# Gate tiles loaded in quarters, and ScalarE's queue loading the second product's first operands

## What is computed

```
def peer_ffn(h, w_q, subkeys, u, v):          # in chunks of tokens ht
    q = (ht @ w_q).reshape(PEER_CHUNK, PEER_HEADS, 2, PEER_HALF)
    s = jnp.einsum('thpc,hpnc->thpn', q, subkeys)
    sv, si = lax.top_k(s, PEER_TOPK)
    ...
    expert = jnp.take_along_axis(cand_i, top_pos, axis=-1)
    gate = jax.nn.softmax(top_s, axis=-1)
    act = jax.nn.gelu(jnp.einsum('thkd,td->thk', u[expert], ht), approximate=False)
    return jnp.einsum('thk,thkd->td', (gate * act), v[expert])
```

## Time and profile before

| | |
|---|---|
| time, median of 3 runs | 2747.01 us (2740.32 to 2752.84) |
| the profiled execution | 2750.26 us, its span 2748.1 us |
| TensorE busy | 2616.9 us, 95% |
| VectorE busy | 2140.3 us, 78% |
| ScalarE busy | 882.0 us, 32% |
| GpSimd busy | 1497.1 us, 54% |
| DMA | 763.30 MB, mean 278 GB/s |

### The profile page before, as it was taken

How to read it: one execution, slowest core, us unless ns; L and a number is a source line. 1 busy time by engine, 2 the same in 40 slices (tenths; PEclk the granted TensorE clock), 3 DMA queues, 4 the chain that set the end, 5 groups by cost and what they waited for, 6 DMA issues and landing times.

```text
span 2748.1 us, 41486 instructions
## 1 busy us (share of the span) xinstructions
PE 2616.9 (95%) x15177; PEld 2345.7 (85%) x15177; DVE 2140.3 (78%) x4568; ACT 882.0 (32%) x1654; POOL 1497.1 (54%) x960
## 2 busy tenths in 40 slices
PE   7999989999999999999999999988999989999988
PEld 6777758999999999989999999966877877878777
DVE  6022273599888999989999994278998988989987
ACT  4223242222122122246666662232222222222222
POOL 1111020346666677776555556546766766867762
PEclk9999999999999999999999999999999999999999
DMA  4110022335777788889999999999999999999995
GB/s 145 46 31 26 21 76 102 114 110 170 271 259 271 270 273 294 288 274 384 375 369 383 381 381 329 329 339 382 386 387 384 391 373 385 390 372 389 382 378 198
DMA packets 294988, 763.30 MB, mean 278 GB/s; under 512 B 24272, under 2 KB 114768, under 8 KB 292048
## 3 DMA queue, kind: packets, MB, share of 16 engines
q0 software_dynamic: 110592, 402.70, 39.2%
q1 hardware_dynamic: 166992, 296.21, 31.7%
q10 hardware_dynamic: 17280, 62.92, 5.9%
HBM read 669.47 MB, written 92.27 MB: 277 GB/s over the span
## 4 chain that ended last, share of the span: by engine, by line
PE 52%; DVE 16%; DMA 12%; issue 5%; POOL 2%; ACT 1%; another core or an unknown queue 0%; DVEq 0%; SPq 0%; ACTq 0%
PE bank L1553 23%; DMA a_raw<-act_d 11%; PE bank L1920 9%; PE wide L1920 8%; PE bank L1891 5%; DVE u_row L1358 4%; PE bank L1819 3%; PE bank L1802 2%; POOL w_lo L653 1%; DVE rest_k L1285 1%; DVE ix L1288 1%; DVE eq L1345 1%; DVE v_lo L1502 1%; DVE ix L1291 1%; DVE top L1286 1%
## 5 line engine op out<-in xcount | busy, mean ns | idle before, releaser
L704 POOL DMA_INDIRECT d_row<-in_v,ids x384 | 632.0, 1646 | 295.6 <-DVE yg L1495 207.6
L1553 PE MATMUL bank<-h_hi,w_hi 128*128 128x320 f32 (+1 forms) x2368 | 563.6, 319 | 14.0 <-POOL w_lo L653 11.9
L653 POOL TENSOR_TENSOR w_lo<-w_raw,w_hi 128x1024 fp32r<-128x1024 f32 x144 | 365.2, 2537 | 336.6 <-ACT w_hi L923 276.4
L1553 PE MATMUL bank<-h_hi,w_lo 128*128 128x320 f32 (+1 forms) x2368 | 547.2, 312 | 0.0
L1553 PE MATMUL bank<-h_lo,w_hi 128*128 128x320 f32 (+1 forms) x2368 | 546.8, 312 | 0.0
L1358 DVE CUSTOM_DVE_ANT_0 u_row<-wide,u_row 128x1024 f32<-128x1024 f32 x384 | 450.3, 1221 | 78.2 <-DMA u_row<-in_u_rows,ids 75.9
L1495 DVE SCALAR_TENSOR_TENSOR yg<-d_row,uh,yg 128x1024 f32<-128x1024 f32 x384 | 474.2, 1280 | 0.0
L662 POOL DMA_INDIRECT u_row<-in_u_rows,ids x384 | 392.9, 1023 | 111.8 <-issue 77.0
L1553 PEld LDWEIGHTS bank<-h_hi,w_hi 128*128 128x128 f32 x2368 | 394.2, 190 | 18.8 <-POOL w_lo L653 13.5
L1553 PEld LDWEIGHTS bank<-h_lo,w_hi 128*128 128x128 f32 x2368 | 400.4, 189 | 2.5
L1553 PEld LDWEIGHTS bank<-h_hi,w_lo 128*128 128x128 f32 x2368 | 399.1, 189 | 2.5
(11 more groups left out here) (227 smaller groups left out, 4267.0 us busy)
## 6 DMA issues: line engine op xcount, KB each, us to landing
w_raw<-in_u SPq DMA_DIRECT2D x128, 512.0 KB
v_raw<-in_v ACTq DMA_DIRECT2D x120, 512.0 KB
act_d<-act_st SPq DMA_DIRECT2D x128, 320.0 KB
g_d<-g_st SPq DMA_DIRECT2D x20, 2048.0 KB
a_raw<-act_d SPq DMA_DIRECT2D x160, 256.0 KB
g_raw<-g_d SPq DMA_DIRECT2D x32, 1024.0 KB
w_raw<-in_w_q SPq DMA_DIRECT2D x32, 512.0 KB
w_raw<-in_w_in SPq DMA_DIRECT2D x20, 512.0 KB
```

Source lines behind the costliest of these rows:

```text
L653: nc.gpsimd.tensor_tensor(w_lo[:, s % 2, :], w_raw[:, s % 2, :], w_hi[:, s % 2, :], ALU.subtract).then_inc(lo_done, 1)
L704: nc.gpsimd.indirect_dma_start(d_row[k % DR][:, :], None, v_rows, bass.IndirectOffsetOnAxis(ids[:, c:c + 1], 0)).then_inc(d_in[k % DR], 16)
L1553: ins = pe.matmul(banks[h][:, 0:n], lhs[:, part], rhs[:, k, h * n:(h + 1) * n], start=(k == 0 and lhs is lhs_hi and rhs is h_hi), stop=(k ...
```

## The change

Gates of tokens 0 to 511 are loaded in four transfers of 256 KB a half, four strips each, where one transfer of 1 MB was (`G_PART` is 4 strips, `G_PARTS` is 4). VectorE waits for all four of a half. In SyncE's loop the quarters of the next group's first half are asked for in steps 4 to 7, those of the second half in steps 8 and 9 and in steps 0 and 1 of the group that uses them; `g_first` in step 3 instead of 2. SyncE no longer loads ahead in the last six bodies of the first product. ScalarE's queue does: its 20 last items are unrolled, and behind each of items 128 to 142, after Gelu and `w_hi`, it issues one step of `fetch`: six units, four quarters, `g_first`, four quarters, one a step, with a `v_raw` ahead of it in steps 0, 1, 5, 6, 10 and 11. The first step waits for the stores of the gates and of the first chunks of `act_d`. The loading functions now take the queue as an argument.

```diff
+        def load_g(queue, g, s, q):
+            j, b = GT * g + VJ * s, G_PART * q
+            if g:
+                queue.wait_ge(pd_done, unit_of(g - 1, VJ * s + VJ - 1) + 1)
+            queue.dma_start(g_raw[s][:, b:b + G_PART, :], g_d[b:b + G_PART, :, j:j + VJ, :]
+                            .rearrange("b p j t -> p b (j t)")).then_inc(g_in[s], 16)
...
                     if n + AR + 1 < N_UNITS:
-                        load_a(n + AR + 1)
-                    if g + 1 < NG:
-                        if u == 2:
-                            load_first(g + 1)
-                        elif u == 4:
-                            load_g(g + 1, 0)
-                        elif u == 8:
-                            load_g(g + 1, 1)
+                        load_a(sp, n + AR + 1)
+                    if g and u < 2:
+                        load_g(sp, g, 1, u + 2)
+                    elif g + 1 < NG and u == 3:
+                        load_first(sp, g + 1)
+                    elif g + 1 < NG and 4 <= u < 8:
+                        load_g(sp, g + 1, 0, u - 4)
+                    elif g + 1 < NG and u >= 8:
+                        load_g(sp, g + 1, 1, u - 8)
...
-            with act.Fori(C0, ITEM_BODIES - 1) as it:
-                for s in range(2):
-                    chunk(it, s)
-            for s in range(2):
-                chunk(ITEM_BODIES - 1, s, ahead=False)
+            def fetch(n):
+                if n == 0:
+                    for k in range(2):
+                        act.wait_ge(g_out[k], 16 * PAIRS)
+                    for k in range(2):
+                        act.wait_ge(act_out[k], 16 * GT // 2)
+                if n % 5 < 2:
+                    act.dma_start(v_raw[:, 2 * (n // 5) + n % 5, :], v[2 * (n // 5) + n % 5, :, :]
+                                  ).then_inc(v_in[2 * (n // 5) + n % 5], 16)
+                if n < AR:
+                    load_a(act, n)
+                elif n < AR + G_PARTS:
+                    load_g(act, 0, 0, n - AR)
+                elif n == AR + G_PARTS:
+                    load_first(act, 0)
+                else:
+                    load_g(act, 0, 1, n - AR - G_PARTS - 1)
+
+            fetches = AR + 2 * G_PARTS + 1
+            chunks = 2 * (ITEM_BODIES - C0)
+            for n in range(chunks):
+                chunk(C0 + n // 2, n % 2, ahead=n + 2 < chunks)
+                if 0 <= n - (chunks - 1 - fetches) < fetches:
+                    fetch(n - (chunks - 1 - fetches))
...
-                        dve.wait_ge(g_in[j // VJ], 16 * (g + 1))
+                        dve.wait_ge(g_in[j // VJ], 16 * G_PARTS * (g + 1))
```

More of the change, by code:

```diff
@@ L67 @@
 RA = 5
+G_PART = 4
+G_PARTS = 4
 UNIT = 512
@@ L450, in build, with load_a, load_first @@
         LO_BANKS = 2 * NT
+        def load_a(queue, n):
+            g, j, f = unit(n)
+            if n >= AR:
+                queue.wait_ge(pd_done, n - AR + 1)
+            if f is None:
+                queue.dma_start(a_raw[:, n % AR, :], act_d[GT * g + j, :, 0:UNIT]).then_inc(a_in[n % AR], 16)
+            else:
+                j0 = GT * g + VJ * f
+                queue.dma_start(a_raw[:, n % AR, :].rearrange("p (j t) -> p j t", j=VJ),
+                                act_d[j0:j0 + VJ, :, FIRST * P:DS].rearrange("j p t -> p j t")
+                                ).then_inc(a_in[n % AR], 16)
+        def load_g(queue, g, s, q):
[4 more added lines that the diff above has]
+                            .rearrange("b p j t -> p b (j t)")).then_inc(g_in[s], 16)
+        def load_first(queue, g):
+            if g:
+                queue.wait_ge(pd_done, first_of(g - 1, 1) + 1)
+            queue.dma_start(g_first[:, :, :], g_d[UNIT // TW:STRIPS, :, GT * g:GT * g + GT, :]
+                            .rearrange("b p j t -> p b (j t)")).then_inc(gf_in, 16)
         @block.sync
@@ L544, in load_v @@
                 sp.dma_start(v_raw[:, j % VR, :], v[j, :, :]).then_inc(v_in[j % VR], 16)
[L546 to L572, removed]
             for it in range(C0, ITEM_BODIES):
@@ L581, in _ @@
                         store_strip(STRIPS - 1)
[L582 to L598, removed]
             store_item(ITEMS - 1)
@@ L611, in _ @@
                 sp.dma_start(y[i][:, :], x1_d[i]).then_inc(y_in, 16)
-            load_a(AR)
+            load_a(sp, AR)
             for g in range(NG):
```

## The result

The changed kernel took 2757.15 us (median of 20 runs, 2748.77 to 2765.48), the kernel before 2743.56 us beside it (20 runs, 2739.53 to 2752.84): a ratio of 1.0046 with a 95% interval of 1.0036 to 1.0056, some 13 us. The forecast was 9 us less. The profiled execution took 2760.79 us, and its span is 10.6 us longer than that of before; the profiled executions lie 6.7 us (before) and 3.6 us (changed) over their medians, so the difference between them is a little small. TensorE is busy as long as it was in the earlier trace rows.

What follows compares the result with a forecast made beforehand. Full DMA engines were taken to bound the second product's groups. Spreading -8.5 us and the items -0.5 us gave -9 us: from a median of 2747.0 to 2738 us, range 2722 to 2760 us.

Steps and rivals of the forecast that it cites:

- the term of -8.5 us for spreading: Groups of the second product: quarters spread over steps save 8.5 us, two thirds of the 12.5 us allowed at most.
- the best pair of neighbours: Group stretches 1953.2 to 2068.1 us: 389.3 GB/s against a mean of 383; at that rate the groups take 805.5 us.
- Nothing moves: Rival, groups of the second product: the rate sets the pauses, quarters only redistribute them, 0 to -2 us, 2746 us; chance 0.12.
- The rival of late quarters: Third and seventh unit of each group: the last quarter comes too late, +25 us, 2772 us; chance 0.11.
- Its threshold: Late quarters decide once the last lands more than 2.4 us after VectorE asks, over 24 us after its issue.
- a queue with less in it: SyncE's queue in the groups: argument against late quarters, beside a byte-set rate and longer pauses giving that queue the engines.
- Its price: Late quarters make each group take 60.2 us, 14 groups 843 us, +25 us.
- The 0.5 us of the items: Last 19 items of the first product: 134.71 us against 133.8; moving first loads off SyncE's queue gains 0.5 us.
- Issue times: Sign of being right: SyncE's units issue in under 5 us, ScalarE's issues take under 0.6 us.
- Some 2.4 us of a VectorE wait are absorbed: Stretch 2007.6 to 2068.1: TensorE misses 3.1 us for VectorE's 5.5, so only a longer wait pauses it.
- Bytes and packets stay: Loop over groups: quarters keep bytes and 512-byte packets, adding only 6 issues, 2.6 us a group, on SyncE.
- The fit of 2.0 us + bytes / 436 GB/s: Skill page's transfer cost: four quarters 10.4 us against 4.4 a half, some 190 us over 32 halves; the trace disagrees.

Runs made afterwards that it cites:

- 7 steps: Changed kernel with all four quarters of a half asked for back to back in steps 4 and 8, g_first in 2: 2743.18 us, 0.9993 of the kernel before.
- 6 steps: Changed kernel with two quarters in each of steps 4, 5, 8 and 9, g_first in 2: 2743.61 us, 0.9995 of the kernel before.
- 5 steps: Changed kernel with only the last quarter of each half one step earlier (steps 6 and 0): 2750.9 us, 1.0021 of the kernel before.
- 3 steps: Changed kernel with every quarter and g_first in the loop one step later: 2769.2 us, 1.0095 of the kernel before.
- half rows: Gathered rows cut to 2 KB in both kernels, VectorE adding that half twice: 2688.88 us in the order before, 2687.97 us in the changed one.

## Why the prediction held in some steps and failed in others

By notice, the ratios line up: 7 steps 0.9993, 6 steps 0.9995, 5 steps 1.0021, 4 steps 1.0046 (1.0035 without ScalarE's part), 3 steps 1.0095. Six and seven are alike; below that a step costs 0.25% at first and 0.5% at the end. **The cause is shown:** the last quarter of each half is asked for in step 7 or in step 1, and SyncE's queue, behind full engines, needs longer than the four steps that are left. The run at notice 5 moves that quarter alone and takes back half of the loss; how the other half divides between the notice and the step of `g_first` is open.

Point by point:

- *Right:* the engines are full (with half rows both orders take 54.4 us a group); ScalarE's issues are hidden (at most 0.67 us, a little over the 0.6 given as a sign, in an item's idle 5.33); the second product starts when it did; small transfers have no cost of their own here. The time, 2757 us, lies inside the range given, near its upper end, but on the other side of the kernel before than was forecast: 9 us less were forecast and 13 more measured. The 0.5% named as what a measurement can tell was too coarse: 0.46% is clear of an interval of 0.1% to either side.
- *The step that failed is the term of -8.5 us for spreading, wrong in sign and in kind.* The quarters in the loop alone cost 0.35% (some 9 us) where they were to bring 8.5. The term took the best pair of neighbours as a rate that a smoother order could hold. Quarters at once and pairs, which differ in the spread and by one step of notice, both stay within 0.1% of the kernel before and still wait 61 and 68 us. The low slices behind the pauses were read as bytes that a smoother order would bring back; no order brought the pauses down. What order can do is lower the rate: 378 GB/s instead of 383. "Nothing moves", at 0.12, is the rival that best describes spreading with a notice of six or seven steps.
- *The rival of late quarters, at 0.11, was the one that came true.* Its place (third and seventh unit) holds, though the waits of before stood there too: the prediction puts both of its two at the third unit, but the one ahead of 2112.47 is at the seventh. Its threshold, a landing over 24 us after the issue, was passed (27.49, 28.88) but was set too high: it took 22 us for four steps, and in group 1 VectorE was ready after 17.8; the chain also runs over a landing of 21.44 us. What failed is the conclusion from "a queue with less in it". The queue did take its transfers more readily; the issues of units in these stretches (min, median and max in ns, with their first and last start) before and now:

```profile
L552 SPq DMA_DIRECT2D a_raw<-act_d x112: 327/673/23377, 1837.9 to 2651.1; - x112
L461 SPq DMA_DIRECT2D a_raw<-act_d x112: 340/571/10419, 1837.7 to 2662.6; - x112
```

But it moves as many bytes a group as before, and in group 1 the quarter still came 9.78 us late: a unit issued 1.84 us behind it took 9.59 us to issue. So a long pause that "gives SyncE's queue the engines alone" didn't save it either.

- *Its price was too high:* +25 us from every group pausing as 2007.6 to 2128.0 did; measured +11.7. Seven of the 14 stretches take 59.8 us or more, but the other seven take 55.3 to 57.9. A long pause is often followed by a short group (61.0, then 55.3; together 116.3, and 116.0 before), which I read as the queues catching up in the pause; that is not shown. One step of notice more or less would have changed the price by half or doubled it (the runs with 5 and 3).
- *The 0.5 us of the items:* measured 134.50 against 134.71 us, too small to tell.
- *Issue times:* SyncE's units were to stay under 5 us; they reach 10.4 us. The waits were to stay under 4 us each; they average 80.0 / 13 = 6.2 us. Groups 2 to 14 were to take 55 to 59.5 us, and six take more; the rate was to be 386 to 390 GB/s, and no slice under 340, where the lowest shown here has 276.
- *"Some 2.4 us of a VectorE wait are absorbed" was misread.* It compares idle time alone. In 2007.6 to 2068.1 TensorE's 241 matmuls took 57.42 us at a granted clock of 0.94, and 54.40 us at 1.00 in 1953.2 to 2007.6; the stretch is 6.1 us longer than the full one, for a VectorE wait of 5.5. So a pause of TensorE brings slower matmuls behind it too: in 1885 to 1890 (below) the granted clock is 0.50, the lower of its two levels, after a slice in which TensorE was busy for 1.52 of 5 us.
- *"Bytes and packets stay":* the bytes do; the packets of the 14 stretches are 163380 instead of 161967, nearly all of the new ones under 512 bytes. Quarters at once have them too and cost nothing.
- *The fit of 2.0 us + bytes / 436 GB/s:* the Trainium skill, "DMA: Bandwidth & Descriptors", gives it in the section "Anatomy of one DMA — SWDGE (gpsimd) path", not in "Bandwidth", and for transfers on GpSimd's path. The quarters go by SyncE's and ScalarE's queues.

How a shorter notice lowers the rate of a stage that moves the same bytes is argued, not shown: during a VectorE wait for gates, no row is added, so no buffer for a row or a `v` comes free, so the engines run out of requests. The slices of the changed kernel that follow such waits agree in part: the rate is low in all three, from 395 GB/s at a share of 1.05 in 1875 to 1880, but the share has fallen only in the second and third (5 us each, columns as above):

```profile
1880.00:1885.00 5.00, 1.52 (x7) 0.94 (x5) 2.54 (x4) 0.63 (x1) 0.00 (x0) 0.92 1.04 320
1885.00:1890.00 5.00, 0.22 (x1) 0.22 (x2) 5.00 (x6) 0.00 (x0) 3.87 (x4) 0.50 0.98 323
...
2395.00:2400.00 5.00, 1.26 (x6) 0.72 (x4) 4.79 (x6) 1.58 (x2) 0.90 (x1) 0.96 0.88 276
```

GpSimd, which asks for the rows, does nothing from 1880 to 1885, TensorE almost nothing from 1885 to 1890. What would have shown it is a version with more buffers for rows at the same notice, which was not run.

## What to carry to other kernels

In a stage that fills the DMA engines, the deadline of an operand is that of its last byte: measure how long the queue takes from issue to landing under load (here 16.5 us in the median and up to 29), and ask for the last part at least that long ahead. Cutting a transfer into parts is safe where the last part is asked for no later than the whole was, and a loss where spreading pushes it back. If no order gives less time, look at the bytes: here a cut in them (which leaves out part of the result) gave 53 us, while none of the nine orders run, the changed kernel's among them, gave any.

## What was not expected of the hardware

- A quarter of 256 KB takes 16.5 us from issue to landing (median, quarters at once) with the engines full, and 5.4 us at a share of about 0.9 beside gathered rows of half the length. The share is an eighth lower and the bytes of the 14 stretches 29% fewer (223.3 MB instead of 313.6); the landing takes a third of the time.
- Four transfers of 256 KB asked for together cost the same as one of 1 MB (0.9993 [0.9984, 1.0002]); the Trainium skill, "DMA: Bandwidth & Descriptors", section "Bandwidth", asks for 1 MB or more a transfer, and with other transfers in flight this run doesn't bear that out.
- The queue that carries the gates is the one that lags. With the gates on ScalarE's, units land in 7.7 us instead of 15.6 and `v` in 14.5 instead of 7.3, at an equal time of the kernel.
